# Two-head attention steps with transposed results, the state-space mixer first, and one shared pair of banks for two modulation vectors

## What is computed

```python
shift1, scale1, gate1, shift2, scale2, gate2 = silu(c) @ w_ada + b_ada      # one set for context, one for latent tokens
h = rmsnorm(x, g_norm1) * (1 + scale1) + shift1
proj = h @ w_in      # columns of mixers A, B (q, k, v), C (z, xbc, dt), D (q, k, v) and of four gates
ya = attention(rope(norm(qa)), [rope(norm(ka)), cache_k], [va, cache_v])    # 4 heads of 64, 2 key/value heads
yb = the same with a window of 128 and a sink logit per head
yc = rmsnorm(ssd(conv(xbc), dt) * silu(z))                                  # state-space mixer, chunks of 128
yd = rmsnorm(softmax(s0) @ v - lam * softmax(s1) @ v)                       # differential attention, 4 heads
x  = x + gate1 * ((sum over the 4 mixers of sigmoid(gate_n) * (y_n @ w_br[n])) @ w_out)
h2 = rmsnorm(x, g_norm2) * (1 + scale2) + shift2
x  = x + gate2 * (16 experts, each takes its 16 context and 32 latent tokens: silu(x @ w1) * (x @ w3) @ w2)
```

## Time and profile before

| | |
|---|---|
| median of 3 runs | 2039.87 us (2039.13 to 2042.09) |
| the profiled execution's own time | 2045.24 us |
| its span, first to last instruction | 2043.5 us |
| PE busy | 1894.9 us (93%), 7750 instructions |
| DVE, ACT, POOL busy | 482.6, 351.9, 50.1 us |
| mean granted TensorE clock | 0.970 of full |
| DMA | 532.98 MB, mean 261 GB/s |

### The profile page before, as it was taken

One profiled execution on the slowest core, in us unless ns is written; L12 is line 12 of the kernel. 1 busy time (PEld: TensorE's weight loads), 2 busy tenths in 40 slices (PEclk: granted clock), 3 DMA queues, 4 the chain that ended last, 5 costly groups with the idle time before them and its releaser, 6 DMA issues.

```text
span 2043.5 us, 19689 instructions
## 1 busy us (share of the span) xinstructions
PE 1894.9 (93%) x7750; PEld 866.6 (42%) x7750; DVE 482.6 (24%) x1249; ACT 351.9 (17%) x916; POOL 50.1 (2%) x91
## 2 busy tenths in 40 slices
PE   6999999999799999898879999999897999999988
PEld 2464444455333433333345644444554334334322
DVE  1033224453411111101020522243524001111101
ACT  2123222421210100100021232223213001001000
POOL 2100000000300000000000000000000000000000
PEclk8999999988899999999989999999888999999999
DMA  9142113245589999999951411133436899999997
GB/s 379 62 158 79 49 55 124 73 179 204 224 339 418 420 428 429 428 428 428 423 231 62 175 62 62 42 124 135 178 143 247 346 426 424 428 428 428 427 429 308
DMA packets 65476, 532.98 MB, mean 261 GB/s; under 512 B 6688, under 2 KB 6816, under 8 KB 41344
## 3 DMA queue, kind: packets, MB, share of 16 engines
q1 hardware_dynamic: 62256, 527.59, 63.1%
q0 software_dynamic: 3152, 4.47, 0.7%
HBM read 529.16 MB, written 2.88 MB: 260 GB/s over the span
## 4 chain that ended last, share of the span: by engine, by line
PE 77%; DMA 15%; DVE 4%; ACT 2%; issue 1%; SPq 0%; ACTq 0%; DVEq 0%
PE bank L588 73%; DMA ring<-in_w_e 14%; PE bank L597 4%; DMA ring<-in_w_ada 1%; ACT scr L1413 1%; DVE x L1919 0%; DVE scr L1624 0%; DVE hT L1487 0%; DVE scr L1856 0%; DVE scr L1853 0%; DVE hT L1485 0%; DVE scr L1794 0%; ACT scr L1400 0%; ACT scr L1402 0%; DVE scr L1788 0%
## 5 line engine op out<-in xcount | busy, mean ns | idle before, releaser
L588 PE MATMUL bank<-ring,hT 128*128 128x512 f32 (+2 forms) x1440 | 597.2, 568 | 2.6 <-DVE hT L1487 2.6
L588 PE MATMUL bank<-ring,scr 128*64 128x512 f32 (+1 forms) x2176 | 529.2, 598 | 44.6 <-DMA ring<-in_w_e 26.3
L588 PE MATMUL bank<-scr 128*64 128x512 f32 (+6 forms) x2048 | 437.2, 520 | 8.1 <-DVE dsm L1763 4.7
L588 PEld LDWEIGHTS bank<-ring,hT 128*128 128x128 f32 x1440 | 268.0, 191 | 270.6 <-issue 264.4
L588 PEld LDWEIGHTS bank<-ring,scr 128*64 128x64 f32 (+1 forms) x2176 | 176.0, 142 | 368.7 <-issue 310.3
L588 PEld LDWEIGHTS bank<-scr 128*64 128x64 f32 (+3 forms) x2048 | 183.0, 164 | 260.6 <-issue 252.2
L597 PE MATMUL bank<-cst,scr 128*128 128x128 f32 (+1 forms) x530 | 94.7, 294 | 47.8 <-ACT scr L1413 24.9
L1411 ACT ACTIVATE scr<-bank 128x512 f32<-128x512 f32 x32 | 19.1, 597 | 674.6 <-PE bank L588 674.6
L1904 DVE TENSOR_TENSOR scr<-scr,bank 128x512 f32<-128x512 f32 x32 | 22.0, 687 | 470.0 <-ACT scr L1411 470.0
L597 PEld LDWEIGHTS bank<-cst,scr 128*128 128x128 f32 (+1 forms) x530 | 63.2, 159 | 111.6 <-issue 76.1
L588 PE MATMUL bank<-ring,csw 128*32 128x512 f32 x384 | 61.1, 782 | 28.4 <-DMA ring<-in_w_ada 17.7
(11 more groups left out here) (217 smaller groups left out, 1037.8 us busy)
## 6 DMA issues: line engine op xcount, KB each, us to landing
ring<-in_w_e SPq DMA_DIRECT2D x124, 2048.0 KB, 18.8
scr<-in_w_e SPq DMA_DIRECT2D x64, 2048.0 KB, 17.6
ring<-in_w_ada SPq DMA_DIRECT2D x24, 2048.0 KB, 9.7
ring<-in_w_in SPq DMA_DIRECT2D x20, 2048.0 KB, 7.8
ring<-in_w_br SPq DMA_DIRECT2D x8, 1024.0 KB, 7.1
ring<-in_w_out SPq DMA_DIRECT2D x4, 2048.0 KB, 8.6
ring<-in_w_in SPq DMA_DIRECT2D x4, 1552.0 KB, 15.9
ring<-in_w_in SPq DMA_DIRECT2D x4, 1536.0 KB, 6.7
```

The costliest lines, as they stand in the source:

```text
L588: ins = pe.matmul(out, lhsT, rhs, start=start, stop=stop, **kw)
```

## The change

It changes four things, in both layers.

1. **Shared tiles for shift and scale.** The adaLN vectors 0 and 1 (and 3 and 4) add into the same pair of banks or rows: `condition(k, second)` shifts the stationary columns by two, so that shift stands in rows 0, 1 and scale in rows 2, 3. `columns` then runs once for the two (16 tiny matmuls fewer in a layer).
2. **State-space mixer first.** Projection C comes first, then D, the conv, and C's chain; the six tiles of projection AB (`ab_unit`) stand between its steps. `rows(3)`, `rows(4)` and `rows(5)` stand there too; `rows(5)` leaves its place behind the output projection. The gates' and lifts' order becomes C, A, B, D. A table (`ORDER`, `HOME`) gives the load order and the slots.
3. **Two heads in a step.** A and B run in 12 steps of two heads (of the two key/value heads) instead of 24 of one. The two score matmuls use rows 0 to 63 and 64 to 127 of the array. The values are stationary (64 columns), the transposed probabilities move (128 columns), and the two heads' results land in the upper and the lower half of bank 6, already transposed: `pair_out` copies them to `boTs`, and the 6 transposes before the lifts of A and B are gone. DVE now scales the probabilities (two instructions of 384 columns) and not the result. A whole gate tile stands in each step.
4. **Expert loads.** The first expert's halves in slots 2 and 3 are issued before those of slots 4, 5, 0 and 1.

```diff
-AT_ADA = (0, 2, 20, 22, 25, 30)
-AT_AB, AT_D, AT_C, AT_OUT = 4, 6, 8, 28
-AT_GATE = (10, 12, 15, 18)
-AT_LIFT = (14, 17, 24, 27)
-LOADS0 = 32
+ORDER = (("ada", 0), ("ada", 1), ("C", 0), ("D", 0), ("ada", 3), ("AB", 0), ("ada", 4), ("ada", 5), ("gate", 0), ("ada", 2),
+         ("gate", 1), ("lift", 0), ("lift", 1), ("gate", 2), ("lift", 2), ("gate", 3), ("lift", 3), ("out", 0))
+HOME = {("ada", 0): 0, ("ada", 1): 2, ("C", 0): 0, ("D", 0): 2, ("ada", 3): 0, ("AB", 0): 0, ("ada", 4): 2, ("ada", 5): 2,
+        ("gate", 0): 2, ("ada", 2): 0, ("gate", 1): 0, ("lift", 0): 2, ("lift", 1): 3, ("gate", 2): 0, ("lift", 2): 2,
+        ("gate", 3): 0, ("lift", 3): 3, ("out", 0): 0}
...
-BRANCH = (0, 1, 3, 2)
+BRANCH = (2, 0, 1, 3)
+AB_UNITS = [(t, b) for b in range(2) for t in range(NT)]
...
+                for s in (2, 3):
+                    half(s, 0)
+                sp.wait_ge(kv_out, (li + 1) * 64)
+                sp.sem_inc(dummy_sp, 1)
                 sp.wait_ge(big, BIG_AT[("up", 3, NT - 1, 1)] + 1)
-                for s in (4, 5, 0, 1, 2, 3):
+                for s in (4, 5, 0, 1):
                     half(s, 0)
 
...
+                bs = [bank(("row", 0, h)) for h in range(2)]
                 for v in range(2):
-
                     j = AT_ADA[v]
-                    bs = [bank(("row", v, h)) for h in range(2)]
                     for c in range(2):
                         need(j + c)
                         for h in range(2):
                             for k in range(4 * c, 4 * c + 4):
                                 q = 32 * (k % 4)
-                                sig = big if k == KD - 1 else freed[j % SLOTS] if h and k == 3 else None
-                                mm(bs[h][q:q + 32, :], csw[:, k, :],
-                                   ring[:, (j + c) % SLOTS, k % 4, h * HALF:(h + 1) * HALF],
-                                   start=c == 0, stop=c == 1, signal=sig)
-                    owed.append(freed[(j + 1) % SLOTS])
+                                sig = freed[SLOT[j]] if h and k == 3 else big if v and k == KD - 1 else None
+                                mm(bs[h][q:q + 32, :], condition(k, v == 1),
+                                   ring[:, SLOT[j + c], k % 4, h * HALF:(h + 1) * HALF],
+                                   start=v == 0 and c == 0, stop=v == 1 and c == 1, signal=sig)
+                    owed.append(freed[SLOT[j + 1]])
                 pe.wait_ge(in_cst0, 16)
-                for v in range(2):
-                    columns(v)
+                pe.wait_ge(sel_ready, 3)
+                columns(0)
...
+                ab_unit(0)
+                decays(0)
+                ab_unit(1)
+                state_scores(0)
+                decays(1)
+                for h in range(2):
+                    rows(4, h)
+                ab_unit(2)
+                state_products(0)
+                state_scores(1)
+                decays(2)
                 columns(3)
-                lift(3)
-                columns(4)
-
+                ab_unit(3)
+                state_products(1)
+                state_scores(2)
+                for h in range(2):
+                    rows(5, h)
+                ab_unit(4)
+                state_products(2)
+                ab_unit(5)
+                pe.wait_ge(h_in, 1)
+                carried(1)
+                carried(2)
...
+                gate0(0)
+                gate0(1)
+                for h in range(2):
+                    rows(2, h)
+                pe.wait_ge(d_ready, 1)
...
+                for s in range(2, 5):
+                    gate0(s)
+                pe.wait_ge(ab_ready, 1)
...
+                def pair_scores(n):
+                    i, g, t = PAIRS[n]
+                    k0, k1 = keys(t)
+                    if n:
+                        pe.wait_ge(p_ready, n)
+                    masked = i == 1 and t > 0
+                    for v in range(2):
+                        rows_ = slice(v * HD, (v + 1) * HD)
+                        mm(banks[4 + v][:, 0:k1 - k0], qT[rows_, i, g, t * P:(t + 1) * P], kT[rows_, i, k0:k1], start=True,
+                           stop=True, signal=s_ready if v and not masked else None, skip_group_check=masked)
+                    if masked:
+                        other = slice(P, 2 * P) if t == 1 else slice(0, P)
+                        for v in range(2):
+                            mm(banks[4 + v][:, other], ident, c_("negabove") if t == 1 else c_("negbelow"), start=False,
+                               stop=True, signal=s_ready if v else None, skip_group_check=True)
+                def pair_weights(n):
+                    i, g, t = PAIRS[n]
+                    pe.wait_ge(w_ready, n + 1)
+                    if n:
+                        pe.wait_ge(pts_ready, n)
+                        pe.wait_ge(o_ready, n)
+                    nb = 3 if t else 1
+                    for v in range(2):
+                        for k in range(nb):
+                            turn(banks[6 + v][:, k * P:(k + 1) * P], pr[:, n % 2, v * T + k * P:v * T + (k + 1) * P],
+                                 signal=pt_ready if v and k == nb - 1 else None)
+                def pair_values(n):
+                    i, g, t = PAIRS[n]
+                    pe.wait_ge(pts_ready, n + 1)
+                    vs = [values(i, v, t) for v in range(2)]
+                    nb = len(vs[0])
+                    for k in range(nb):
+                        for v in range(2):
+                            mm(banks[6][v * HD:(v + 1) * HD, T:512], vs[v][k], pT[:, v, k * P:(k + 1) * P], start=k == 0,
+                               stop=k == nb - 1, signal=pv_ready if v and k == nb - 1 else None, skip_group_check=True)
...
+                def turned(i):
+                    pe.wait_ge(bo_ready, 1 if i == 0 else 2)
+                    src = sz if i == 0 else bo
+                    for c in range(2):
+                        b = bank(("boT", i, c))
+                        for t in range(NT):
+                            turn(b[:, t * P:(t + 1) * P], src[:, t, c * P:(c + 1) * P], signal=big if t == NT - 1 else None)
+                def lift(i, t):
+                    j = AT_LIFT[i]
+                    if t == 0:
+                        if i in (0, 3):
+                            taken(("boT", i, 1))
+                        else:
+                            pe.wait_ge(o_ready, i * NP // 2)
+                        need(j)
+                    for h in range(2):
+                        b = bank(("up", i, t, h))
+                        for c in range(2):
+                            mm(b[:, :], boTs[i][:, c, t * P:(t + 1) * P], ring[:, SLOT[j], c, h * HALF:(h + 1) * HALF],
+                               start=c == 0, stop=c == 1, signal=big if c == 1 else None)
+                    if t == NT - 1:
+                        owed.append(freed[SLOT[j]])
+                for n in range(NP):
+                    i, s = 1 + n // (NP // 2), n % (NP // 2)
+                    if n == NP // 2:
+                        for t in range(NT):
+                            lift(0, t)
+                    pair_scores(n)
+                    gate(i, s, 0)
+                    if n:
+                        pair_weights(n - 1)
+                    gate(i, s, 1)
+                    if n == NP // 2 - 1:
+                        turned(0)
+                    if n:
+                        pair_values(n - 1)
+                scores(0)
+                pair_weights(NP - 1)
+                lift(1, 0)
+                pair_values(NP - 1)
+                for t in (1, 2):
+                    lift(1, t)
+                for n in range(NIT + 2):
+                    if 1 <= n < NIT:
+                        scores(n)
+                    if 1 <= n <= NIT:
+                        weights(n - 1)
+                    if n >= 2:
+                        weighted(n - 2)
+                    if 1 <= n <= NIT:
+                        gate(3, (n - 1) // 2, (n - 1) % 2)
+                for t in range(2):
+                    lift(2, t)
+                turned(3)
+                lift(2, 2)
+                for t in range(NT):
+                    lift(3, t)
...
-                for h in range(2):
-                    rows(5, h)
...
+                def pair_turned(n):
+                    i, g, t = PAIRS[n]
+                    nk = T if t else P
+                    act.wait_ge(pt_ready, n + 1)
+                    if n:
+                        act.wait_ge(pv_ready, n)
+                    for v in range(2):
+                        ins = A(pT[:, v, 0:nk], banks[6 + v][:, 0:nk], ACT.Copy)
+                    ins.then_inc(pts_ready, 1)
+                for n in range(NP):
+                    i, g, t = PAIRS[n]
+                    nk = T if t else P
+                    q = 2 * (n % 4)
+                    act.wait_ge(m_ready, n + 1)
+                    for v in range(2):
```

(34 more changed lines are left out.)

1005 lines of the change are left out of this document (495 added, 510 removed).

## The result

The changed kernel takes 1984.73 us (median of 4, 1981.02 to 1987.07) where the kernel before takes 2039.96 (median of 4): a ratio of 0.973 (95% interval 0.971 to 0.974), 55.2 us less. The forecast was 1987, with a range of 1968 to 2018.

The account below looks back on a forecast made before the run. PE was taken to bound the mixers and loads the experts, so the first expert's start sets the time. Terms sum to -26.9 us per layer, -53.8 in all: from the 2039.87 median 1986, stated as 1987, range 1968 to 2018.

Parts of the forecast that it names:

- Scores -8.4: Mixers A and B: score matmuls of two heads in different array rows cost what one costs, -8.4 us per layer.
- Values -3.5: Value matmuls of A and B: the two column halves of the array work at once, -3.5 us per layer.
- Transposes -1.9: Twelve transposes go, at 0.16 us each: -1.9 us per layer.
- Columns at the start -1.0: Start of a layer: 8 of 16 small column matmuls go, half the gain kept, -1.0 us per layer.
- last columns -2.0: The last `columns` (3.66 us) goes, but DVE's last two adds now show: -2.0 us per layer.
- `rows(5)` +3.6: Moves from the output projection's end, where it was free, into the state-space stretch: +3.6 us per layer.
- the clock ahead of `h2T` +2.5: New idle stretch ahead of `h2T` slows its 24 transposes and a little of the router: +2.5 us per layer.
- Waits -7.7: PE's waits in state-space mixer, first score chain, A, B and D: 10.7 us gone, 3 put back, net -7.7 per layer.
- The norms: Head norms of A and B, and of D, fit under new cover; `ab_ready` about 1 us before PE asks.
- Clock -8.5: State-space mixer and last lift: of 13.3 us lost to low clock some 4 remain; -8.5 us per layer, least-known term.
- The first rival: Whole kernel: only the matmuls that go are won, waits and clock come back; 2014 to 2019 us, chance 0.28 with its kin.
- the one on the other side: C's stretch: small matmuls keep PE at the lower clock, dense tiles at half speed; +66 us per layer, 2170; slower 0.05.

Follow-up runs that it names:

- experiment 4: Changed kernel with half a gate tile placed between the score matmuls of the two heads: 2005.2 us against 1984.7.
- experiment 3: Changed kernel with the value matmuls of one head behind each other, then the other head's, instead of alternating: 1988.7 us against 1984.7.
- experiment 1: Changed kernel with `rows(5)` put back behind the output projection, load order and expert-half order changed with it: 1971.0 us against 1984.7.
- experiment 2: Changed kernel with all six AB tiles in one piece ahead of the first decays, none between the state-space steps: 1998.9 us against 1984.7.
- Experiment 7: Changed kernel with one gate tile ahead of the transposes of the cached keys: 1977.3 us against 1984.7.
- experiment 11: Kernel of experiments 8 with ACT's square root for the norm of A and B moved ahead of its part of the gate tile: 1964.0 us.
- experiment 12: Kernel of experiment 11 with `columns(3)` moved between the fifth AB tile and the products of tile 2: 1969.3 us.
- experiments 8: Changed kernel with `rows(5)` behind the output projection and a gate tile ahead of the cached keys' transposes: 1966.0 us against 1984.7.
- 10: Kernel of experiments 8 with `columns(3)` behind the fourth AB tile and ACT's square root for A and B's norm ahead of its gate tile: 1965.6 us.
- experiments 9: Changed kernel with `columns(3)` behind the fourth AB tile instead of ahead of it, nothing else: 1988.5 us against 1984.7.

## Why the prediction was right

The frame held: PE bounds the mixers, the loads bound the experts, and the first expert starts earlier by what PE saves. In layer 0 that is 26.0 us (27 forecast). In layer 1 the mixer part became 32.2 us shorter (559.6 to 527.4), 6.2 more than in layer 0. Its larger pieces are 3.1 us of clock that the changed kernel loses in C's stretch of layer 0 and not in that of layer 1, 1.2 at the layer's turn, and about 1.9 that mixers A, B and D of the kernel before took longer there (210.4 against 208.5). None of these differences was in the sum, which was worked out for layer 0 and doubled.

- **Scores -8.4**: two in 0.84 us; experiment 4 shows that this is the overlap of neighbours.
- **Values -3.5**: eight steps of 0.81 and four of 0.37 us are 8.0 for 11.6 us, -3.6. Of the two bounds the lower one was right, for the reason taken (experiment 3).
- **Transposes -1.9**: left out as forecast; no experiment of their own.
- **Columns at the start -1.0, last columns -2.0**: projections start 1.45 us earlier in layer 0 (40.22 against 41.67), and `mT` 3.52 - 1.51 = 2.0 us. In layer 1 the projections start 2.6 us sooner behind the experts (27.2 in place of 29.8 us); there the 24 transposes of before had run partly at the lower level (5.34 us, 4.30 in layer 0).
- **`rows(5)` +3.6 and the clock ahead of `h2T` +2.5**: right in sign, place and size; the last stage is 2.3 us longer, and experiment 1 gives both back. The Trainium skill ("TensorE: Matmul & The Clock Gate", "Why this matters for your kernels") advises against idle gaps between bursts of matmuls. The trace agrees: behind 5.31 us of idle time the transposes ran at the lower level, behind `rows(5)` and 1.75 us of idle time at the upper one. The same page's rule that transposes don't count as PE work (Part 4) is not needed for it: behind `rows(5)` the same 24 transposes kept the upper level through 3.23 us.
- **Waits -7.7**: 12.4 us became 2.25 + 1.64 + 0.71 + 0.78 = 5.4, so -7.0. The size was right and the reason only half. The text put the products' waits down to the AB tiles that now stand before them; experiment 2 takes these away and the products still don't wait (0.8 us comes ahead of the carried states). More than half of the 7.1 us of C's stretch stood at the norm of C's result and at the copies of `boT` (2.3 and 1.6 us, experiment 2), and a mixer lies over C's norm and copy now. What covers the products' own 2.3 us stays open. Put back were 1.5 us at the last lifts (of 3 forecast, with C's copy at nothing). The wait of 2.25 us for the cached keys was not foreseen.
- **The norms**: `ab_ready` comes at 223.55 us and PE asks at 230.28, 6.7 us to spare and not 1. Experiment 7 used that up by having ACT take the norm's square root one gate tile later; with it ahead of the tile (experiment 11) the wait is gone.
- **Clock -8.5**: in layer 0 about 13.3 us lost became 3.1 (0.04 x 76.4) and 1.7 (0.03 x 55.7), right. In layer 1 the kernel before had lost more (0.88 and 0.76 in its two stretches, 7.8 + 6.1 us) and the changed one loses 0 in the same 76.4 us. That is one execution each: in layer 1 the fall behind `columns(3)` is there in some profiles and not in others (experiment 12).

The profiled executions differ by 61.3 us (2045.24 and 1983.94), the medians by 55.2; the sum was 53.8. The execution shown of before lay 5.3 us above its median, that of after 0.8 below. How much of these 6 us is the clock's coming and going in layer 1 stays open. That 1987 lies within 3 us of the median is therefore partly luck: the sum for two layers was 7.5 us too small for the executions that it was read from and compared with. The first rival (only the matmuls that go are won, 2014 to 2019) and the one on the other side (a low clock through the whole C stretch) did not occur: C's stretch has no wait, and a clock of 0.96 and 1.00.

## What to carry to other kernels

Where PE works in order and another part is bound by loads, look for work that needs nothing and keep it for the place where PE must wait anyway: `rows(5)` was free in its old place and cost 6.5 us a layer in its new one, and the versions that put it back and fill the wait for the cached keys (experiments 8, 10 and 11) are the fastest here, 1964 to 1966 us. Two heads in different halves of the array cost what one costs only if they stand side by side; with other work between them the gain is gone. When a wait disappears in a reordering, take the supposed cover away before crediting it: here the waits stayed away without the tiles between the steps, whose worth lay in the clock and a load.

## What was not expected of the hardware

The 8 matmuls of `columns(3)`, 4 columns each and 3.67 us in all, are followed by the lower level of PE's clock in 20 of the 26 profiled layers in which they stand, though PE is not idle around them: behind a dense tile of 7.03 us at full clock the next products took 3.68 us in place of 2.00 (experiments 9 and 12, both layers). What it is about them no run here tells. And two value matmuls that follow each other in the same column half take 0.21 us each, where two in different halves take 0.27 together.
